# Turning the gated feed-forward rows: VectorE blocks and a DRAM scratch in place of TensorE transposes

## The chip, the core and the metric

One Trainium2 chip, one core. The metric is device time in microseconds (us), the median of the runs of a kernel. The kernel before took 1355.84 us, median of 3 runs (1354.32 to 1356.59).

## The reference, cut to what matters

The model runs two blocks of two layers each on 256 rows of 1024 numbers, all in float32. The change touches the last part of each layer of the second block, the feed-forward:

```python
D_MODEL = 1024; SEQ = 256; DEPTH = 2; D_FF = 2816
def swiglu(h, w_gate, w_up, w_down):
    return (jax.nn.silu(h @ w_gate) * (h @ w_up)) @ w_down
# second block, for l in range(DEPTH), after the mixer has been added to x:
#   x = x + rms_norm_2(swiglu(rms_norm_2(x, ffn_pre[l]), gate[l], up[l], down[l]), ffn_post[l])
```

`silu(h @ w_gate) * (h @ w_up)` is 256 rows by 2816 columns. TensorE sums over the partition axis, so for the product with `w_down` these gated rows have to stand with their 2816 columns on the partitions: they have to be turned.

## The kernel before, in words

**Weights.** TensorE's work is cut into weight units of 4 slices of 128 rows by 512 columns (1 MiB), loaded one after the other by SyncE's queue into a ring of `SLOTS` = 4 places; only the two units of the first group, F0, are staged elsewhere. The load of a unit waits until TensorE has used the unit four places earlier (`w_used`, L590 to L611). ScalarE then rounds a unit in two halves (`round_weights`, L1177), and VectorE subtracts to get the rest of each half (`weight_rests`, L1579). Every product is three matmuls of 512 columns: rounded by rounded, rounded by rest, rest by rounded. One unit is 2 row tiles x 4 slices x 3 = 24 matmuls (L669).

**Feed-forward.** It has 11 groups F0 to F10 (`FF_G` = 11) of two units each: 256 gate columns and 256 up columns, two DMAs of 512 KB to a unit. After group j ScalarE applies silu to the gate half (L1547), VectorE multiplies it with the up half into `sg[:, j % 2]` (L2319), TensorE turns `sg` in four 128x128 transposes into one PSUM bank (step `fh{j}`, L637), ScalarE rounds that bank into `hid_hi[:, j]` (L1538, `turned`) and VectorE writes `hid_rest[:, j]` (`turned_rest`, L1579). The transposes of group j-1 stand between the two units of group j. The groups E0 and E1 (six units each, `w_down`) then multiply `hid_hi` and `hid_rest` by the down weights; unit c of E0 uses what groups 2c and 2c+1 gave.

**Orders.** The order on each engine is written out by hand. In round j ScalarE rounds the weights up to the second unit of group j+1 (`AHEAD` = 2), then does `turned(j-2)`, then silu of group j; VectorE follows with `weight_rests`, `turned_rest(j-2)`, the multiplication. Two pairs of PSUM banks alternate between groups, so group j+2 may start only when group j has been read. SyncE issues the loads in the order of the units, each behind its wait; what stands in its order before a load holds that load back. The first units of F0 and F1 run row tile by row tile, so F0 ends late and F1 5.5 us after it.

Of the kernel before, what the change touches and what calls it, by code (L numbers as in the profile page):

```python
# [7 lines left out]
P = 128  # L8
S = 256
TT = S // P  # L10
D = 1024
KD = D // P
DEPTH = 2
# [7 lines left out]
FF_G = D_FF // 256  # L21
KF = D_FF // P
UNIT_K = 4
SLOTS = 4
# [84 lines left out]
for _n, _name in enumerate(("do_g", "mq_g", "mk_g", "ho_g")):  # L109
# [11 lines left out]
    + ["kT0", "kT1", "mm0", "mm1", "at0", "at1", "mi"] \  # L121
    + [step for n in range(1, len(LEVELS)) for step in [f"Y{n}"] + [f"T{n}"] * (n > 1) + [f"Z{n}"] + BETWEEN.get(n, [])] \
    + ["oT_r0", "oT_r1", "u0", "wT", "st", "vn1", "do0", "do1", "oT_d0", "oT_d1"] \
    + [f"yT{i}" for i in range(4)] + [f"fT{i}" for i in range(4)] + [f"fh{j}" for j in range(FF_G)]
PRE = ["colM", "memT0", "memT1", "memT2", "memT3", "colA", "colB"]
STEPS = PRE + [f"A{l}.{s}" for l in range(DEPTH) for s in ORDER_1] + [f"B{l}.{s}" for l in range(DEPTH) for s in ORDER_2]
STEP_NO = {s: n for n, s in enumerate(STEPS)}
# [57 lines left out]
def parts_until(u):  # L185

    return sum(1 for v, _, _ in PARTS if v <= u)
# [17 lines left out]
def last_unit(group):  # L205
    return max(u for u, (g, _, _) in enumerate(UNITS) if g == GROUP_NO[group])
# [8 lines left out]
def mixer_program(nc, w, out):  # L215
    F = mybir.dt.float32
    FR = mybir.dt.float32r
    ALU = mybir.AluOpType
    ACT = mybir.ActivationFunctionType
    X = mybir.AxisListType.X  # L220
    ctx = ExitStack()
    with ctx:
# [3 lines left out]
        def sem(name):  # L226
            return ctx.enter_context(nc.semaphore(name))
# [39 lines left out]
        def region(at, *shape):  # L267
            n = int(np.prod(shape))
            assert at + n <= ARENA
            v = arena[:, at:at + n]  # L270
            if len(shape) == 1:
                return v
            names = "abcd"[:len(shape)]
            return v.rearrange(f"p ({' '.join(names)}) -> p {' '.join(names)}",
                               **{c: s for c, s in zip(names[:-1], shape[:-1])})
# [36 lines left out]
        R2 = {g: 1024 * n for n, g in enumerate(names_2)}  # L312
# [5 lines left out]
        b_tmp, b_mx, b_pw, b_gf = take(1024), take(1024), take(512), take(1024)  # L318
# [23 lines left out]
        xs2 = region(b_e, TT, D)  # L342
        sq2 = region(b_e, 2048)
        sg = region(b_tmp, 2, 2, S)


        def part(name, at, *shape):
# [20 lines left out]
        hid_hi, hid_rest = part("hid_hi", R2["RV"], FF_G, 2, S), part("hid_rest", R2["RV"] + FF_G * 2 * S, FF_G, 2, S)  # L368
# [40 lines left out]
        pow_asked, pow_given = sem("pow_asked"), sem("pow_given")  # L409
        v_chain, a_chain = sem("v_chain"), sem("a_chain")  # L410
        out_done = sem("out_done")
        w_rounded, w_split = sem("w_rounded"), sem("w_split")
        named = {}
        pow_widths = []

        def sig(name):
            if name not in named:
                named[name] = sem(name)
            return named[name]

        def computed(step):
            return step_done, STEP_NO[step] + 1

        def read_out(step):
            return step_read[STEP_NO[step] % 4], STEP_NO[step] // 4 + 1

        def bank(step, *dims):
            v = mp[:, STEP_NO[step] % 4]
            if len(dims) == 2:
                n = dims[0] * dims[1]  # L430
                return v[:, 0:n].rearrange("p (a b) -> p a b", a=dims[0])
            return v[:, 0:dims[0]] if dims else v
# [10 lines left out]
        def taken(group):  # L443
            return group_read[GROUP_NO[group] % 2], GROUP_NO[group] // 2 + 1
# [99 lines left out]
        def load_signal(u):  # L544
            return staged_loaded[staged_half(u)] if u in STAGED_UNITS else w_loaded[slot_of(u)]

        def load_place(u):
            return ("staged", staged_half(u)) if u in STAGED_UNITS else ("ring", slot_of(u))

        place_total = collections.Counter()  # L550
        unit_value = []
        for u in range(len(UNITS)):
# [4 lines left out]
        def _(sp):  # L557
# [6 lines left out]
            for u in range(1, len(UNITS)):  # L564
# [23 lines left out]
                if u in STAGED_UNITS:  # L588
                    l, g = int(GROUPS[UNITS[u][0]][0][1]), GROUPS[UNITS[u][0]][0][3:]
# [19 lines left out]
                    sp.dma_start(const[:, c0:c1], w["shape_constants"][:, c0:c1]).then_inc(loaded["const2"], 16)  # L609
                for dst, src in unit_loads(u):  # L610
                    sp.dma_start(dst, src).then_inc(load_signal(u), 16)  # L611
            for t in range(TT):
                sp.wait_ge(sig("x_tile"), 2 * (3 * DEPTH) - TT + t + 1)
                sp.dma_start(out[0, t * P:(t + 1) * P, :], x[:, t, :]).then_inc(out_done, 16)
# [4 lines left out]
        def _(pe):  # L619
# [14 lines left out]
            def transposes(step, tiles, *waits):  # L634
                begin(step, *waits)
                for j, tile in enumerate(tiles):
                    last = nc.tensor.transpose(bank(step)[:, P * j:P * j + P], tile, ident)  # L637
                end(last)
# [34 lines left out]
            def split_units(group, count, halfway=None, tile_ready=None):  # L673

                for _ in range(count):
                    u = state["unit"]
                    g, k0, _ = UNITS[u]
                    assert GROUPS[g][0] == group
                    state["unit"] += 1
                    if k0 == k_ends(group)[0] and g >= 2:  # L680
                        pe.wait_ge(group_read[g % 2], g // 2)
                    for n in range(parts_until(u - 1), parts_until(u)):
                        if halfway is not None and n > parts_until(u - 1):
                            halfway()
                        split_part(n, range(TT), tile_ready).then_inc(w_used, 1)
# [240 lines left out]
            for l in range(DEPTH):  # L926
                s = lambda n: f"B{l}.{n}"

                def group_in(g):
                    n = GROUP_NO[s(g)]  # L930
                    return group_read[n % 2], n // 2 + 1
# [169 lines left out]
                                   (1, 1, "halfway"): lambda: tile_transposes(s("fT"), DEPTH + 2 * l + 1, 0)})  # L1101
                rows_first(s("fT"), DEPTH + 2 * l + 1)

                def hid_transposes(j):
                    transposes(s(f"fh{j}"), [sg[:, j % 2, t, P * c:P * c + P] for c in range(2) for t in range(TT)], group_in(f"F{j}"))
                hid_transposes(0)
                split_units(s("F2"), 1)
                hid_transposes(1)
                split_units(s("F2"), 1)
                for j in range(3, FF_G):  # L1110
                    split_units(s(f"F{j}"), 1)
                    hid_transposes(j - 1)
                    split_units(s(f"F{j}"), 1)
                for c in range(-(-KF // UNIT_K)):
                    for j in range(2 * c, min(2 * (c + 1), FF_G)):
                        pe.wait_ge(*read_out(s(f"fh{j}")))
                    split_units(s("E0"), 1)
                    if c == 0:
                        hid_transposes(FF_G - 1)
                split_units(s("E1"), -(-KF // UNIT_K) - SLOTS)  # L1120
                split_tail(SLOTS, {(1, 2, "halfway"): lambda: tile_transposes(f"B{l + 1}.xT", DEPTH + 2 * l + 2, 0)} if l + 1 < DEPTH else {})
            assert state["unit"] == len(UNITS) and state["step"] == len(STEPS)
# [3 lines left out]
        def _(act):  # L1126
# [243 lines left out]
            for l in range(DEPTH):  # L1370
# [163 lines left out]
                result((s("M0"), s("M1")), DEPTH + 2 * l, next_units(s("F0")),  # L1534
                       lambda t: h_round(s("fT"), col("ffn_pre", l), t, hT_hi))
                def turned(j):
                    act.wait_ge(*computed(s(f"fh{j}")))
                    nc.scalar.activation(hid_hi[:, j], bank(s(f"fh{j}"), 2, S), ACT.Copy).then_inc(sig("turned"), 1)  # L1538
                for j in range(FF_G):
                    round_weights(parts_until(last_unit(s(f"F{j}")) + AHEAD))  # L1540
                    if j > 1:
# [5 lines left out]
                        ins = nc.scalar.activation(sg[:, j % 2, t], group_bank(s(f"F{j}"), t)[:, 0:S], ACT.Silu, scale=row_scale[:, t:t + 1])  # L1547
                    ins.then_inc(sig("ff_sig"), 1)
                turned(FF_G - 2)
                turned(FF_G - 1)  # L1550
                round_weights(parts_until(last_unit(s("E1"))))
                if l + 1 < DEPTH:
# [7 lines left out]
        def _(dve):  # L1560
# [7 lines left out]
            def evac(ins, step):  # L1568
                ins.then_inc(step_read[STEP_NO[step] % 4], 1)
                dve.wait_ge(*read_out(step))  # L1570
# [7 lines left out]
            def sub(o, i0, i1):  # L1578
                return nc.vector.tensor_tensor(o, i0, i1, ALU.subtract)  # L1579
# [17 lines left out]
            def weight_rests(count):  # L1597
                while halved[0] < count:
                    u, k, nk = PARTS[halved[0]]
                    dve.wait_ge(w_rounded, halved[0] + 1)  # L1600
                    sub(rest_of(u)[:, k:k + nk, :], raw_of(u)[:, k:k + nk, :], rounded_part(u)[:, k:k + nk, :].bitcast(F))\
                        .then_inc(w_split, 1)
                    halved[0] += 1
# [426 lines left out]
            for l in range(DEPTH):  # L2030
# [275 lines left out]

                def turned_rest(j):
                    dve.wait_ge(sig("turned"), FF_G * l + j + 1)
                    evac(sub(hid_rest[:, j], bank(s(f"fh{j}"), 2, S), hid_hi[:, j].bitcast(F)), s(f"fh{j}"))
                for j in range(FF_G):  # L2310
                    n = s(f"F{j}")
                    weight_rests(parts_until(last_unit(n) + AHEAD))
                    if j > 1:
                        turned_rest(j - 2)
                    dve.wait_ge(sig("ff_sig"), FF_G * l + j + 1)
                    if j == 0:
                        dve.wait_ge(sig("x_normed"), 2 * (DEPTH + 2 * l + 1) + TT)
                    for t in range(TT):
                        ins = nc.vector.scalar_tensor_tensor(sg[:, j % 2, t], group_bank(n, t)[:, S:2 * S], row_scale[:, t:t + 1],  # L2319
                                                             sg[:, j % 2, t], ALU.mult, ALU.mult)  # L2320
                    ins.then_inc(group_read[GROUP_NO[n] % 2], 1)
                    dve.wait_ge(*taken(n))
                turned_rest(FF_G - 2)
                turned_rest(FF_G - 1)
                weight_rests(parts_until(last_unit(s("E1"))))

# [40 lines left out]
```

## Time and profile before

| what | value |
|---|---|
| median of 3 runs | 1355.84 us |
| profiled execution, span from first to last instruction | 1352.6 us |
| TensorE matmul busy | 1340.9 us (99%) |
| VectorE busy | 935.8 us (69%) |
| ScalarE busy | 746.4 us (55%) |
| DMA, mean busy share of 16 engines | 0.51, 167 GB/s |
| TensorE's granted clock | 0.999 of full speed |

The profile page gives for the profiled execution the span and no other time; the median of the runs lies 3.2 us above it. Busy time of matmuls has modelled ends; for the pace of TensorE the starts are what counts. The chain of work that ended last is followed back from the last instruction, and its pieces are given in order of time.

### The profile page before, as it was taken

How to read it: one execution, taken by the hardware profiler on the slowest of the kernel's cores; microseconds unless marked ns; L12 is line 12 of the kernel's file. 1: busy time of each engine (PE TensorE's matmuls, PEld its weight loads, DVE VectorE, ACT ScalarE, POOL GpSimd, SP SyncE). 2: the span in 40 equal slices, each digit the busy share in tenths (PEclk: the TensorE clock that was granted, in tenths of full speed). 3: DMA queues.
4: the chain of work that ended last, by engine and by line, in shares of the span. 5: the costliest groups of instructions: out<-in, count | busy, mean ns of one | idle time of the engine just before them, and what ended most of it. 6: DMA issues, size and time to landing. Idle time of an engine off the chain costs nothing.

```text
span 1352.6 us, 17955 instructions
## 1 busy us (share of the span) xinstructions
PE 1340.9 (99%) x7129; PEld 1146.8 (85%) x7129; DVE 935.8 (69%) x1214; ACT 746.4 (55%) x1067; POOL 58.2 (4%) x44
## 2 busy tenths in 40 slices
PE   9999999999999999999999999999999999999998
PEld 7988888978888998888878888889888887888886
DVE  6789866699867488757885555457695778655544
ACT  6864766675674565544465444456644445544432
POOL 1002000001100001000000000000100000000000
PEclk9999999999999999999999999999999999999999
DMA  8654235554345455434464655644644345466552
GB/s 292 216 168 156 94 125 187 178 165 156 109 148 181 160 198 174 156 118 150 156 218 128 186 186 171 233 156 160 207 156 136 128 157 187 137 206 187 187 176 104
DMA packets 139715, 226.25 MB, mean 167 GB/s; under 512 B 8113, under 2 KB 54897, under 8 KB 139505
## 3 DMA queue, kind: packets, MB, share of 16 engines
q1 hardware_dynamic: 137968, 222.49, 50.1%
q10 hardware_dynamic: 1664, 2.63, 0.5%
q8 instruction: 57, 0.93, 0.3%
q14 instruction: 26, 0.21, 0.1%
HBM read 224.05 MB, written 1.05 MB: 166 GB/s over the span
## 4 chain that ended last, share of the span: by engine, by line
PE 95%; DVE 2%; ACT 1%; issue 1%; DMA 0%; SPq 0%; ACTq 0%; DVEq 0%
PE gp L669 73%; PE gp L657 8%; PE mp L637 5%; PE mp L982 3%; PE mp L798 1%; DVE wt_rest L1579 1%; PE mp L865 1%; PE mp L840 1%; PE mp L975 1%; PE mp L819 1%; PE mp L826 1%; ACT first_hi L1177 1%; DMA wt<-in_w_mem_kv 0%; DVE arena L1573 0%; DVE arena L1576 0%
## 5 line engine op out<-in xcount | busy, mean ns | idle before, releaser
L1579 DVE TENSOR_TENSOR wt_rest<-wt,wt_hi 128x1024 fp32r<-128x1024 f32 x148 | 174.4, 1221 | 83.0 <-ACT wt_hi L1177 81.3
L1177 ACT ACTIVATE wt_hi<-wt 128x1024 fp32r<-128x1024 f32 x148 | 148.1, 1053 | 97.1 <-DMA wt<-in_ffn_down 48.5
L1177 ACT ACTIVATE mix_hi<-wt 128x1024 fp32r<-128x1024 f32 x128 | 132.1, 1060 | 103.7 <-PE gp L669 74.7
L1579 DVE TENSOR_TENSOR wt_rest<-wt,mix_hi 128x1024 fp32r<-128x1024 f32 x128 | 151.1, 1221 | 35.1 <-ACT mix_hi L1177 34.1
L1579 DVE TENSOR_TENSOR wt_rest<-wt,first_hi 128x1024 fp32r<-128x1024 f32 x104 | 124.0, 1221 | 25.8 <-ACT first_hi L1177 24.9
L669 PE MATMUL gp<-mix_hi,mix_hT_hi 128*128 128x512 f32 x352 | 139.9, 397 | 0.0
L669 PE MATMUL gp<-wt_rest,mix_hT_hi 128*128 128x512 f32 x352 | 137.1, 390 | 0.0
L669 PE MATMUL gp<-mix_hi,mix_hT_rest 128*128 128x512 f32 x352 | 133.4, 390 | 0.0
L669 PE MATMUL gp<-wt_hi,hT_hi 128*128 128x512 f32 x320 | 126.7, 396 | 0.0
L1177 ACT ACTIVATE first_hi<-wt 128x1024 fp32r<-128x1024 f32 x104 | 105.8, 1059 | 36.9 <-PE gp L669 26.1
L669 PE MATMUL gp<-wt_hi,hT_rest 128*128 128x512 f32 x320 | 124.9, 390 | 0.0
L669 PE MATMUL gp<-wt_rest,hT_hi 128*128 128x512 f32 x320 | 124.6, 389 | 0.0
L2344 POOL TENSOR_TENSOR rs_out<-rs_in,minus_half 128x1 f32<-128x1 f32 (+3 forms) x35 | 53.8, 1539 | 1289.5 <-DVE rs_in L1584 1289.5
L1137 ACT ACTIVATE arena<-gp 128x1024 f32<-128x1024 f32 x50 | 51.3, 1026 | 95.3 <-PE gp L669 95.3
L669 PE MATMUL gp<-first_hi,first_hT_hi 128*128 128x512 f32 x256 | 103.4, 404 | 0.2 <-DVE wt_rest L1579 0.2
L669 PE MATMUL gp<-first_hi,first_hT_rest 128*128 128x512 f32 x256 | 99.9, 390 | 0.0
L669 PE MATMUL gp<-wt_rest,first_hT_hi 128*128 128x512 f32 x256 | 99.8, 390 | 0.0
L669 PEld LDWEIGHTS gp<-mix_hi,mix_hT_rest 128*128 128x128 f32 x352 | 66.1, 188 | 14.1
L669 PEld LDWEIGHTS gp<-mix_hi,mix_hT_hi 128*128 128x128 f32 x352 | 66.2, 188 | 13.5 <-DVE wt_rest L1579 0.8
L669 PEld LDWEIGHTS gp<-wt_rest,mix_hT_hi 128*128 128x128 f32 x352 | 66.2, 188 | 12.7
L637 PE MATMUL mp<-const,arena 128*128 128x128 f32 x568 | 75.5, 276 | 0.6 <-DVE arena L1576 0.4
L637 PEld LDWEIGHTS mp<-const,arena 128*128 128x128 f32 x568 | 66.4, 142 | 10.6 <-issue 3.0
(347 smaller groups left out, 2933.6 us busy)
## 6 DMA issues: line engine op xcount, KB each, us to landing
wt<-in_w_in SPq DMA_DIRECT2D x96, 1024.0 KB, 5.1
wt<-in_w_out SPq DMA_DIRECT2D x20, 1024.0 KB, 5.1
wt<-in_ffn_gate SPq DMA_DIRECT2D x40, 512.0 KB, 4.0
wt<-in_ffn_up SPq DMA_DIRECT2D x40, 512.0 KB, 5.0
wt<-in_ffn_down SPq DMA_DIRECT2D x20, 1024.0 KB, 5.1
wt<-in_w_mem_kv SPq DMA_DIRECT2D x7, 1024.0 KB, 5.2
arena<-in_w_in SPq DMA_DIRECT2D x4, 1024.0 KB, 8.1
wt<-in_w_branch_pool SPq DMA_DIRECT2D x4, 1024.0 KB, 5.0
```

Source lines behind the costliest of these rows:

```text
L637: last = nc.tensor.transpose(bank(step)[:, P * j:P * j + P], tile, ident)
L657: last = nc.tensor.matmul(o, a[:, k, P * c:P * c + P], b[:, :, k0 + k, :], start=(k0 + k == 0 and c % 2 == 0 and i == 0), stop=(k0 + k == ...
L669: last = nc.tensor.matmul(group_bank(group, t), a, b[:, k, :], start=(kk == k_first and i == 0), stop=(kk == k_last and i == 2))
L798: last = nc.tensor.matmul(bank(step)[:, P * h:P * h + P], keys(h), queries(h), start=True, stop=True)
L819: end(nc.tensor.matmul(b[:, P:3 * P], QT[:, h, P:S], KT[:, h // 2, :], start=True, stop=True))
L826: last = nc.tensor.matmul(bank(s(f"ms{h}"), TT, MEM)[:, t, :].rearrange("p (a b) -> p a b", a=TT), reg("A", "QM")[:, t, P * h:P * h + P], ...
L840: last = nc.tensor.matmul(bank(s(f"om{t}"))[:, P * h:P * h + P], mprT[:, h, 2 * t + st, :], reg("A", "VM")[:, st, P * h:P * h + P], start= ...
L982: last = nc.tensor.matmul(bank(step)[:, P * h:P * h + P], lhs(h), rhs(h), start=True, stop=True)
L1137: nc.scalar.activation(dst, group_banks(name), func).then_inc(group_read[GROUP_NO[name] % 2], 1)
L1177: nc.scalar.activation(rounded_part(u)[:, k:k + nk, :], raw_of(u)[:, k:k + nk, :], ACT.Copy)\
L1579: return nc.vector.tensor_tensor(o, i0, i1, ALU.subtract)
L2344: nc.gpsimd.tensor_tensor(rs_out[:, at:at + width], rs_in[:, at:at + width], minus_half[:, 0:width], ALU.pow)\
```

## The change

The 11 steps `fh{j}` of each layer go, with their four TensorE transposes each. In their place, for each group j of a layer:

- VectorE, after its multiplication, turns `sg[:, j % 2]` (128 by 512) in blocks of 32 by 32 into `turned_h[:, j % 2]` with one instruction.
- SyncE writes `turned_h` (256 KB) to `hid_far` in DRAM in rows of 512 bytes, waits for that, and issues four reads of 64 KB that bring the blocks to their places in `hid_raw[:, j]`, in pieces of 128 bytes. All this stands in SyncE's order right behind the load of the second unit of group j+2.
- ScalarE and VectorE take their rounding and rest from `hid_raw` in SBUF. The rest is written over `hid_raw`.
- E0's unit c waits for VectorE's rests (`hid_split`). For the last group both engines first do the weights of two more units.

```diff
+        turned_h = region(b_mx, 2, 2, TT, P)
+        hid_raw = region(R2["RV"] + FF_G * 2 * S, FF_G, 2, S)
+        hid_far = nc.dram_tensor("hid_far", (DEPTH * FF_G, 2 * TT, P, P), F, kind="Internal").ap()
...
+        hid_after = {last_unit(f"B{l}.F{j}") + SLOTS: FF_G * l + j for l in range(DEPTH) for j in range(FF_G)}
...
                 for dst, src in unit_loads(u):
                     sp.dma_start(dst, src).then_inc(load_signal(u), 16)
+                if u in hid_after:
+                    n = hid_after[u]
+                    l, j = divmod(n, FF_G)
+                    sp.wait_ge(sig("hid_turned"), n + 1)
+                    sp.dma_start(hid_far[n].rearrange("m q c -> q m c"), turned_h[:, j % 2].rearrange("q c t i -> q (c t) i"))\
+                        .then_inc(hid_out, 16)
+                    sp.wait_ge(hid_out, 16 * (n + 1))
+                    far = hid_far[n].rearrange("m (p i) (j r) -> j i (m p) r", p=4, j=4)
+                    near = hid_raw[:, j].rearrange("q c s -> q (c s)").rearrange("q (b r) -> q b r", r=32)
+                    for q in range(4):
+                        sp.dma_start(near[32 * q:32 * q + 32], far[q]).then_inc(hid_back, 16)
...
-                hid_transposes(0)
-                split_units(s("F2"), 1)
-                hid_transposes(1)
-                split_units(s("F2"), 1)
-                for j in range(3, FF_G):
-                    split_units(s(f"F{j}"), 1)
-                    hid_transposes(j - 1)
-                    split_units(s(f"F{j}"), 1)
+                for j in range(2, FF_G):
+                    split_units(s(f"F{j}"), 2)
                 for c in range(-(-KF // UNIT_K)):
-                    for j in range(2 * c, min(2 * (c + 1), FF_G)):
-                        pe.wait_ge(*read_out(s(f"fh{j}")))
+                    pe.wait_ge(sig("hid_split"), FF_G * l + min(2 * (c + 1), FF_G))
                     split_units(s("E0"), 1)
-                    if c == 0:
-                        hid_transposes(FF_G - 1)
...
                 def turned(j):
-                    act.wait_ge(*computed(s(f"fh{j}")))
-                    nc.scalar.activation(hid_hi[:, j], bank(s(f"fh{j}"), 2, S), ACT.Copy).then_inc(sig("turned"), 1)
+                    act.wait_ge(hid_back, 16 * 4 * (FF_G * l + j + 1))
+                    nc.scalar.activation(hid_hi[:, j], hid_raw[:, j], ACT.Copy).then_inc(sig("turned"), 1)
...
                 turned(FF_G - 2)
+                round_weights(parts_until(last_unit(s(f"F{FF_G - 1}")) + SLOTS))
                 turned(FF_G - 1)
...
-                    evac(sub(hid_rest[:, j], bank(s(f"fh{j}"), 2, S), hid_hi[:, j].bitcast(F)), s(f"fh{j}"))
+                    sub(hid_rest[:, j], hid_raw[:, j], hid_hi[:, j].bitcast(F)).then_inc(sig("hid_split"), 1)
...
                     dve.wait_ge(*taken(n))
+                    if FF_G * l + j > 1:
+                        dve.wait_ge(hid_out, 16 * (FF_G * l + j - 1))
+                    nc.vector.transpose(turned_h[:, j % 2].rearrange("q c t i -> q t c i"), sg[:, j % 2].rearrange("q t (c i) -> q t c i", c=2))\
+                        .then_inc(sig("hid_turned"), 1)
                 turned_rest(FF_G - 2)
+                weight_rests(parts_until(last_unit(s(f"F{FF_G - 1}")) + SLOTS))
                 turned_rest(FF_G - 1)
```

## Rows read from the trace of the kernel before

**Rows 1.** The page: busy time by engine, and the chain's shares by engine.
```profile
PE 1340.9 (99%) x7129; PEld 1146.8 (85%) x7129; DVE 935.8 (69%) x1214; ACT 746.4 (55%) x1067; POOL 58.2 (4%) x44
...
PE 95%; DVE 2%; ACT 1%; issue 1%; DMA 0%; SPq 0%; ACTq 0%; DVEq 0%
```

**Rows 2.** The chain in order of time, layer 0's feed-forward: start us, us, what.
```profile
724.70 0.44 PE mp L637 x4
...
742.42 10.94 PE gp L669 x48
753.36 0.44 PE mp L637 x4
...
832.89 0.44 PE mp L637 x4
833.33 46.74 PE gp L669 x206
```

**Rows 3.** Timeline of SyncE's queue, same stretch: start us, us, engine line, DMA.
```profile
722.00 0.37 SPq L611 DMA_DIRECT2D wt<-in_ffn_gate  x1
...
724.73 0.37 SPq L611 DMA_DIRECT2D wt<-in_ffn_gate  x1
...
730.66 0.37 SPq L611 DMA_DIRECT2D wt<-in_ffn_gate  x1
...
736.57 0.37 SPq L611 DMA_DIRECT2D wt<-in_ffn_gate  x1
...
747.94 0.37 SPq L611 DMA_DIRECT2D wt<-in_ffn_gate  x1
748.35 0.51 SPq L611 DMA_DIRECT2D wt<-in_ffn_up  x1
```

**Rows 4.** Timeline of ScalarE, same stretch, with idle time before and its releaser.
```profile
719.29 0.84 ACT L1547 ACTIVATE arena<-gp,small 128x256 f32<-128x256 f32 x2 [5.28 <-PE gp L669]
...
736.58 0.84 ACT L1547 ACTIVATE arena<-gp,small 128x256 f32<-128x256 f32 x2 [3.65 <-PE gp L669]
...
742.01 2.01 ACT L1177 ACTIVATE wt_hi<-wt 128x1024 fp32r<-128x1024 f32 x2 [2.70 <-DMA wt<-in_ffn_up]
```

**Rows 5.** Timeline of VectorE, the multiplication of group 2.
```profile
737.52 0.88 DVE L2319 SCALAR_TENSOR_TENSOR arena<-gp,small,arena 128x256 f32<-128x256 f32 x2 [3.04 <-ACT arena L1547]
```

**Rows 6.** VectorE's groups by form: count | busy us, mean ns of one | idle before.
```profile
L1579 DVE TENSOR_TENSOR wt_rest<-wt,wt_hi 128x1024 fp32r<-128x1024 f32 x148 | 174.4, 1221 | 83.0 <-ACT wt_hi L1177 81.3 <-DVE arena L2319 0.4
...
L2319 DVE SCALAR_TENSOR_TENSOR arena<-gp,small,arena 128x256 f32<-128x256 f32 x44 | 19.3, 479 | 67.1 <-ACT arena L1547 67.1
...
L1579 DVE TENSOR_TENSOR hid_rest<-mp,hid_hi 128x512 fp32r<-128x512 f32 x22 | 15.1, 685 | 8.1 <-ACT hid_hi L1538 8.1
```

**Rows 7.** The DMA view of 748 to 753 us: rate in 40 slices of 0.125 us.
```profile
GB/s 0 0 0 0 0 0 0 25 82 74 8 41 33 16 131 279 369 336 336 385 385 385 385 385 385 377 385 385 385 377 393 393 385 377 352 303 148 58 25 8
```

**Rows 8.** Stretches: us, busy by engine, clock, DMA share, GB/s: queued loads; output store.
```profile
725.00:729.00 4.00, 4.00 (x20) 3.29 (x19) 1.98 (x4) 2.12 (x4) 0.00 (x0) 1.00 1.06 357
...
1341.00:1342.00 1.00, 1.00 (x7) 0.81 (x6) 0.00 (x0) 0.00 (x0) 0.00 (x0) 1.00 1.00 410
```

**Rows 9.** Page, DMA issues: count, KB each, median us from issue to landing.
```profile
wt<-in_ffn_up SPq DMA_DIRECT2D x40, 512.0 KB, 5.0
...
out<-x SPq DMA_DIRECT2D x2, 512.0 KB, 2.6
```

**Rows 10.** The two loads of w_ba: second issue in the queue's timeline, then their landings.
```profile
29.49 0.43 SPq L587 DMA_DIRECT2D w_ba<-in_w_in  x1
...
DMA to landing us min/median/max: 2.8/5.0/7.2
```

**Rows 11.** The DMA view of 26.9 to 27.6 us, then of 30.5 to 32 us.
```profile
DMA packets 955, 0.07 MB, mean 99 GB/s; under 512 B 937, under 2 KB 954, under 8 KB 955
...
q1 hardware_dynamic: 955, 0.07, 92.2%
...
q1 hardware_dynamic: 1245, 0.09, 73.2%
```

More of the change, by code:

```diff
@@ L123 @@
     + ["oT_r0", "oT_r1", "u0", "wT", "st", "vn1", "do0", "do1", "oT_d0", "oT_d1"] \
-    + [f"yT{i}" for i in range(4)] + [f"fT{i}" for i in range(4)] + [f"fh{j}" for j in range(FF_G)]
+    + [f"yT{i}" for i in range(4)] + [f"fT{i}" for i in range(4)]
 PRE = ["colM", "memT0", "memT1", "memT2", "memT3", "colA", "colB"]
@@ L411, in mixer_program @@
         out_done = sem("out_done")
+        hid_out, hid_back = sem("hid_out"), sem("hid_back")
         w_rounded, w_split = sem("w_rounded"), sem("w_split")
@@ L1102, in _ @@
                 rows_first(s("fT"), DEPTH + 2 * l + 1)
-                def hid_transposes(j):
-                    transposes(s(f"fh{j}"), [sg[:, j % 2, t, P * c:P * c + P] for c in range(2) for t in range(TT)], group_in(f"F{j}"))
-                hid_transposes(0)
-                split_units(s("F2"), 1)
-                hid_transposes(1)
-                split_units(s("F2"), 1)
-                for j in range(3, FF_G):
-                    split_units(s(f"F{j}"), 1)
-                    hid_transposes(j - 1)
-                    split_units(s(f"F{j}"), 1)
+                for j in range(2, FF_G):
+                    split_units(s(f"F{j}"), 2)
                 for c in range(-(-KF // UNIT_K)):
-                    for j in range(2 * c, min(2 * (c + 1), FF_G)):
-                        pe.wait_ge(*read_out(s(f"fh{j}")))
+                    pe.wait_ge(sig("hid_split"), FF_G * l + min(2 * (c + 1), FF_G))
                     split_units(s("E0"), 1)
-                    if c == 0:
-                        hid_transposes(FF_G - 1)
                 split_units(s("E1"), -(-KF // UNIT_K) - SLOTS)
```

## The prediction

> **What bounds the kernel now.** I read the page first, then the chain of waits in order of time through one feed-forward, then the timelines of SyncE's queue, ScalarE and VectorE over the same stretch, last the DMA views. The page says that TensorE is the bound: busy 99% of the span, and 95% of the chain that ended last [rows 1]. The chain through the feed-forward shows nothing but matmuls and, once a group, a piece of 0.44 us for four transposes; no wait of TensorE stands in it [rows 2]. So a TensorE instruction removed here is time removed, provided that its weights still come in time. The reader is to see two things: what a block of transposes costs in pace, and how much air SyncE's queue and the DMA engines have, for they take over the work.
>
> **What is removed.** 48 matmuls take 48 x 46.74/206 = 10.89 us where nothing stands between them (the long piece of E0 and E1), and a group with its transposes takes 10.94 + 0.44 = 11.38 us, from 742.42 to the next group's 753.79 [rows 2]. One block so costs 0.44 (its piece) to 0.49 (the difference of the groups); I take 0.47. There are 11 a layer, the first at 724.70 and the last at 832.89 [rows 2], 22 in all: 22 x 0.47 = 10.4 us, all on the path. The waits of E0 for what was turned were not on the chain and get looser or tighter without a cost, as shown below.
>
> **What VectorE gets.** One instruction of 128x512 a group. The trace has no such operation; the nearest rows are the subtraction of 128x512 at 0.685 us and that of 128x1024 at 1.221 [rows 6]. I take 0.7, by the size; 1.2 is the other end. VectorE had over 2 us of idle before its multiplication and more before the weights' rests [rows 5, 6], so 22 x 0.7 = 15 us vanish beside TensorE. What matters is when it ends: silu starts at the group's end, the multiplication ends 1.82 us later (736.58 to 737.52 + 0.88) [rows 4, 5], the turn at +2.6. ScalarE's and VectorE's rounding and rest keep their size; that they read SBUF now is worth nothing I can see, 0 to 0.1 us each, off the path.
>
> **What SyncE's queue gets, and who waits for it.** This is the dear part. For each group: the wait for the turn, a write of 256 KB (512 packets of 512 B, 32 an engine), the wait for its landing, four reads (2048 packets of 128 B, 128 an engine). Queued behind them on SyncE is the load of group j+3's first unit, due at half of group j+1 (before: 722.00, 724.73, 730.66, 736.57 [rows 3]), then its second unit, then the next write. Since write and reads wait for a landing and SyncE does nothing else meanwhile, the feed-forward gets a second pace: the cycle from the landing of one write to that of the next. TensorE needs 10.89 us a group. The terms of the cycle, in one line of DMAs:
>
> - From issue to first data: 0.95 us (issued 747.94, first slice with data the eighth of 748 to 753 [rows 3, 7]).
> - The four reads. The smallest packets in the trace are those of w_ba: rows of 8 numbers, 32 B, 1024 a load. In a full queue 955 packets took 0.922 x 16 x 0.7 = 10.3 us of engine, 10.8 ns each; in the second stretch 0.732 x 16 x 1.5 = 17.6 us for 1245, 14.1 ns [rows 11]. A 1 KB packet in a full queue moves at 357 GB/s, 1024 x 16/357 = 45.9 ns [rows 8]. So a 128 B packet lies between 10.8 and 45.9 ns. I take 15, near the row of small packets, with room for its 96 B more (4 ns at the full rate): 128 x 15 = 1.9 us. Issuing four takes 4 x (0.43 + 0.05) = 1.9 us by w_ba's second issue, which had landed 2.8 us after [rows 10]. Issue and data overlap all but the last: 2.5 us. Ends: 1.9 and 5.9.
> - Two units of weights: 2.1 MB at 357 GB/s [rows 8], 5.9 us. A lone unit is worse (its two DMAs ramp up for 1.9 us [rows 7]), but these stand in a full queue.
> - The write: 512 B packets, between 10.8 and 45.9 ns, so 0.35 to 1.5 us; I take 31 ns, 1.0 us. Landing after its last data: the output's store of 512 KB lands at 2.6 us [rows 9], of which 0.52/0.41 = 1.3 is data [rows 8] and 0.95 start: 0.4.
> - Handing over between waits: 0.1.
>
> Sum: 0.95 + 2.5 + 5.9 + 1.0 + 0.4 + 0.1 = 10.85 us, beside TensorE's 10.89. With both low ends it is 9.6, with both high ends 14.75. So by my values the cycle just keeps up, and the result hangs on a few tenths of a microsecond.
>
> The Trainium skill gives a reason against the 15 ns: DMA: Bandwidth & Descriptors, section Specifications, names 512 B as the smallest transfer for line rate and says that below it the engine reads, modifies and writes. The rows of w_ba show packets of 32 B into SBUF without a price of that kind, so on them the trace does not agree; a 128 B one is in no row. What it would cost is a rival below.
>
> **The margin at the start.** F0's silu starts at 719.29 [rows 4], its turn ends at about 721.9, and SyncE sits in that wait while F1's loads' places come free: group 3's units go out at 726.1 and 727.1 where it was 722.00 and 724.73. The first write has the queue to itself: 0.95 + 1.0 + 0.4, landed at 724.2. The next lands one cycle later, 724.2 + 10.85 = 735.1. From a write's landing to group j+3's first half ready: 0.95 + 2.5 + 2.95 (one unit) + 0.8 (landing after data: 753.35 by issue and 5.0 [rows 3, 9], data until 752.6 [rows 7]) + 1.0 rounding (half of 2.01 [rows 4]) + 1.22 rest [rows 6] + 0.1 = 9.5 us. So group 4 is ready at 744.6. TensorE, without transposes, starts group 2 at 724.7 and group 4 at 746.5: 1.9 us of margin. Group 3: 724.2 + 9.5 = 733.7 against 735.6, the same 1.9. In the E0 stage the same rule holds until its fifth unit, which stands behind the last reads; after it SyncE is free. So for a cycle c the loss of a layer is about 11 x (c - 10.87) - 1.9 us, where positive: nine cycles of drift, the first cycle, and the part of c in the 9.5. It starts at c = 11.04 and eats the 5.2 us gain of a layer at c = 11.5.
>
> **What else is late.** silu of group j stands behind the rounding of group j+1's second unit and behind turned(j-2). The unit lands about 1 us before the write of j-1 does (0.9 us of write data and 0.4 landing less its own 0.8), its rounding, rest, the multiplication and the turn take some 5.7 us, and the next write's turn in the queue comes 9.3 us after the landing: 3 us of air. The reads of j-2 land a cycle earlier: no wait. The last group's come about 10 us after TensorE's F10 ends and are ready at +12; E0 wants them in its sixth unit, at 5 x 5.45 = +27. Nothing is lost there. If they came over 15 us later it would cost their excess.
>
> **The sum.** In the profiled execution's terms 1352.6 - 10.4 = 1342.2 us of span; the runs' median lies 3.2 above the span, so 1345.4. For drift in some groups I add 0.6: **1346 us**. Its own range is 1344.5 (a block at 0.49 and noise) to 1350 (c = 11.25, 2.3 lost a layer).
>
> **Rivals.**
> 1. *SyncE's round trip paces the feed-forward: slower than before.* Place: TensorE waits for the weights' rests at the start of groups 5 to 10 and of E0's units. It decides from c = 11.5. Price at c = 12.2, which is 128 B packets at 22 ns and a write of 1.4 us: 11 x 1.33 - 1.9 = 12.7 a layer, 25.5 - 10.4 = 15 slower: 1371 us. For it: SyncE's waits in series, and w_ba's second load, at 1.4 us for half as many packets. Against: the small packets at 10.8 ns when queued, and that DMA is busy for only about 0.6 of a group now.
> 2. *Nearly as rival 1, but short of it:* c from 11.25 to 11.5, 1350 to 1356 us.
> 3. *Packets of 128 B cost what 1 KB ones do,* 45.9 ns, and the write too: c = 14.75, 11 x 3.88 - 1.9 = 40.8 a layer, 81.6 - 10.4 = 71 slower, 1427 us. Against: 10.8 ns for smaller ones. This is what the rule of the skill's page on transfers below 512 B would come to.
> 4. *The transposes go and the time does not:* matmuls around them get slower by as much, 1356 us. Against: 48 matmuls without a block run at 10.89 in the same trace.
>
> **Chances.** Forecast 0.45, rival 2 0.15, rival 1 0.30, rival 3 0.05, rival 4 0.05. 0.2% is 2.7 us, about what a measurement can tell from no change: faster is below 1353.1 and takes the forecast and two thirds of rival 2, 0.55; the same takes the rest of it, rival 4 and the edge of rival 1 (c up to 11.63), 0.13; slower 0.32. The range, 1344.5 to 1369, leaves out rival 3 and the worse half of rival 1.
>
> **What would show it.** In the chain, pieces of 96 and more matmuls without a break and 10.9 us from one silu to the next: the removal. In SyncE's timeline the distance of two writes to the scratch: 10.9 by the forecast, over 11.5 by rival 1, and then idle time of TensorE put down to VectorE's rests in groups 4 to 10. Landing of the reads: 3 to 4 us from the first one's issue; over 6 speaks for rival 3. VectorE's turn: 0.7 us. The forecast is wrong if the cycle is longer than 11.3 us or the write's landing takes over 2 us beyond its place in the queue.

## The result and the profile after

The changed kernel takes 1361.91 us, median of 4 runs (1357.51 to 1362.32), beside 1355.08 for the kernel before (1353.99 to 1356.59) in the same job: ratio 1.0046, 95% interval 1.0034 to 1.0059. It is slower by 0.5%, where 0.7% faster was forecast. In a second job it took 1358.75 us, median of 6 runs (1358.34 to 1359.23), ratio 1.0032, interval 1.0020 to 1.0045. So its slowdown is 6.8 us in one job and 4.4 in the other.

The page after, to be read beside [rows 1]: span, busy times, and the chain's shares.

```profile
span 1360.4 us, 17863 instructions
...
PE 1336.7 (98%) x7041; PEld 1137.8 (84%) x7041; DVE 949.9 (70%) x1236; ACT 746.8 (55%) x1067; POOL 58.2 (4%) x44
...
PE 79%; DMA 10%; DVE 4%; SPq 3%; ACT 2%; issue 1%; ACTq 0%; DVEq 0%
```

88 matmuls are gone (7129 to 7041), as the change says. But the chain no longer runs through TensorE alone: 10% of it is DMA and 3% SyncE's queue, where both had 0% [rows 1]. The chain in order of time shows where. Two cycles of layer 0 (start us, us, what):

```profile
754.67 6.38 DMA hid_far<-arena
...
761.07 0.33 SPq L627
...
763.56 0.49 SPq L616
...
765.19 7.97 DMA wt<-in_ffn_up
...
773.18 1.07 ACT wt_hi L1182
...
774.27 2.23 DVE wt_rest L1585 x2
...
776.55 0.68 DVE hid_rest L1585
777.23 0.80 DVE arena L2325 x2
778.06 0.72 DVE arena L2331
...
778.80 7.00 DMA hid_far<-arena
```

Before there were 10.94 us of matmuls and 0.44 of transposes in turn [rows 2]. Now the chain of layer 0's feed-forward goes round a ring without TensorE in it, from 719.90 to 832.15 us: landing of a write, four reads (L627), loads of weights (L616), landing, rounding, rest, the multiplication, the turn (L2331), the next write. That is rival 1. VectorE's turn stands in this ring, but it does not set the pace: the write that follows it lands 6.38 and 7.00 us after its issue, where the first one, with nothing queued before it, landed 2.28 us after (722.45 to 724.73), and in e2 below the same turn stands before the same write and TensorE waits for nothing. Two lines from the waits of the whole execution (waiting engine <- releaser: us in total, times, longest us) say what TensorE and SyncE waited for:

```profile
PE gp L685 <- DVE wt_rest L1585: 14.4, 18, 2.3
...
SPq L627 <- DMA hid_far<-arena: 134.3, 22, 7.7
```

SyncE stood 134 us in its 22 waits for a write, with loads behind them. Against e2 below, matmul for matmul, TensorE falls 9.4 us behind in the feed-forward and down groups of layer 0 and 8.2 us in those of layer 1, and 1.3 us in all the rest. SyncE's timeline in layer 0, beside [rows 3]:

```profile
722.45 0.37 SPq L621 DMA_DIRECT2D hid_far<-arena  x1
724.75 1.94 SPq L627 DMA_DIRECT2D arena<-hid_far  x4
726.73 0.49 SPq L616 DMA_DIRECT2D wt<-in_ffn_gate  x1
...
738.14 1.92 SPq L627 DMA_DIRECT2D arena<-hid_far  x4
...
749.79 1.92 SPq L627 DMA_DIRECT2D arena<-hid_far  x4
...
761.07 2.44 SPq L627 DMA_DIRECT2D arena<-hid_far  x4
...
844.27 1.92 SPq L627 DMA_DIRECT2D arena<-hid_far  x4
```

The reads start when a write has landed, so their distance is the cycle: (844.27 - 724.75)/10 = 11.95 us in layer 0, and 11.85 in layer 1 (1187.67 to 1306.12), mean 11.90, against 10.85 forecast and TensorE's 10.89. Single cycles run from 11.0 to 13.7 us.

### The profile page after: what moved, and what is told of

Its sections match the earlier page's. It is cut to its first block, busy times and chain, and to the rows that moved or that the text cites. A ratio compares the mean times of both kernels' runs of the same rounds, so it can differ in the third digit from the quotient of the medians.

```text
span 1360.4 us, 17863 instructions
## 1 busy us (share of the span) xinstructions
PE 1336.7 (98%) x7041; PEld 1137.8 (84%) x7041; DVE 949.9 (70%) x1236; ACT 746.8 (55%) x1067; POOL 58.2 (4%) x44
## 4 chain that ended last, share of the span: by engine, by line
PE 79%; DMA 10%; DVE 4%; SPq 3%; ACT 2%; issue 1%; ACTq 0%; DVEq 0%
PE gp L685 57%; PE gp L673 8%; DMA hid_far<-arena 5%; PE mp L653 4%; DMA wt<-in_ffn_up 4%; PE mp L998 3%; DVE wt_rest L1585 2%; SPq L627 2%; PE mp L814 1%; SPq L616 1%; DMA wt<-in_ffn_down 1%; PE mp L881 1%; ACT wt_hi L1182 1%; PE mp L856 1%; DMA wt<-in_w_mem_kv 1%
## 5 line engine op out<-in xcount | busy, mean ns | idle before, releaser
L685 PE MATMUL gp<-wt_hi,hT_hi 128*128 128x512 f32 x320 | 126.1, 394 | 10.2 <-DVE wt_rest L1585 10.0
L685 PEld LDWEIGHTS gp<-wt_hi,hT_hi 128*128 128x128 f32 x320 | 60.1, 188 | 27.8 <-issue 15.9
L685 PE MATMUL gp<-wt_hi,hid_hi 128*128 128x512 f32 x176 | 69.1, 393 | 2.2 <-DVE wt_rest L1585 2.2
```

What stands on the lines that cost most here:

```text
L685: last = nc.tensor.matmul(group_bank(group, t), a, b[:, k, :], start=(kk == k_first and i == 0), stop=(kk == k_last and i == 2))
```

## The experiments

The kernels ran in three jobs, each with the kernel before beside them; its median was 1354.2 to 1354.4 us in each, so times are compared across them. "Span" is that of the profiled execution. "Cycle" is the mean distance between the first reads after one write and those after the next, over both layers, from the profile, as above. Where it is under TensorE's 10.89 us, TensorE sets the pace and the cycle does not.

| kernel | us | ratio, 95% interval | span, us | cycle, us |
|---|---|---|---|---|
| changed, again (a2) | 1358.75 | 1.0032 (1.0020 to 1.0045) | 1356.9 | 11.73 |
| e1 no DMA path | 1344.11 | 0.9925 (0.9910 to 0.9939) | 1341.6 | none |
| e2 wait and reads later | 1343.57 | 0.9919 (0.9902 to 0.9935) | 1341.5 | 10.45 |
| e3 reads in 512 B | 1352.35 | 0.9985 (0.9975 to 0.9994) | 1349.3 | 11.40 |
| e4 one read | 1343.80 | 0.9919 (0.9905 to 0.9934) | 1341.9 | 10.51 |
| e5 path beside transposes | 1359.10 | 1.0036 (1.0023 to 1.0050) | 1357.1 | 11.75 |
| e6 only reads later | 1351.97 | 0.9983 (0.9974 to 0.9992) | 1350.7 | 11.36 |
| e7 reads in 64 B | 1379.10 | 1.0183 (1.0168 to 1.0198) | 1378.6 | 12.62 |
| e8 blocks on the write | 1348.64 | 0.9960 (0.9947 to 0.9974) | 1346.1 | 11.14 |
| e9 e6, weights first | 1350.73 | 0.9973 (0.9962 to 0.9984) | 1350.4 | 11.34 |
| e2 again (b4), 5 rounds | 1344.05 | 0.9924 (0.9911 to 0.9936) | 1342.2 | 10.45 |

My theory: the load of group j+3 stands on SyncE behind a write's landing and four reads, and this series is the pace. The rival: the DMA engines carry too much in the feed-forward, wherever the wait stands. A second rival: the price of small packets.

**e1, the saving alone.** VectorE turns straight into `hid_raw`; the write, the wait for it and the four reads are left out.

```diff
-                if u in hid_after:
-                    ...                          # the write, the wait and the four reads
-                    act.wait_ge(hid_back, 16 * 4 * (FF_G * l + j + 1))
+                    act.wait_ge(sig("hid_turned"), FF_G * l + j + 1)
-                    nc.vector.transpose(turned_h[:, j % 2]...)
+                    nc.vector.transpose(hid_raw[:, j].rearrange("q c (t i) -> q t c i", t=TT), ...)
```

> VectorE turns straight into hid_raw; the write to DRAM and the four reads are left out, so the blocks are not permuted and the output is not the reference's. This prices the removed transposes alone. Theory (series wait: the load of group j+3 stands on SyncE behind a write's landing and four reads) and its rival (the DMA engines carry too much, wherever the wait stands) both say that TensorE's 22 blocks x 0.47 us are gained in full: 10.4 us under the kernel before, 1344.7 us, 1343.5 to 1346, no wait of TensorE for the rests in the feed-forward. A third theory, that matmuls lose what the transposes gave, says 1355.

Measured 1344.11 us, as expected, 10.2 under the kernel before. The price of 0.47 us a block held, and the 22 turns on VectorE took nothing of it back. Rival 4, that the matmuls lose what the transposes gave, falls.

**e2, the wait behind the next load.** The same traffic in the same groups.

```diff
                     sp.dma_start(hid_far[n]...).then_inc(hid_out, 16)
+                if u - 1 in hid_after:
+                    n = hid_after[u - 1]
+                    j = n % FF_G
                     sp.wait_ge(hid_out, 16 * (n + 1))
                     far = hid_far[n]...
```

> As the changed kernel with all of its traffic; only the wait for the write's landing and the four reads move on SyncE behind the load of group j+3's first unit. Series wait: that load goes out at its old time, the margin no longer shrinks, the full gain returns: 1345 to 1347 us, TensorE waits under 1 us in all in the feed-forward. Rival, load of the DMA engines: the same bytes and packets meet in the same groups, so it stays at 1358 to 1362 us with TensorE waiting some 12 us.

Measured 1343.57 us: as fast as without the path, and 1.4 us under the expectation of 1345 to 1347. The expectation stood on the forecast's full gain of 1345.4 us, which was too high (see "From span to time" below). The chain of e2 is one piece again through layer 0's feed-forward:

```profile
719.88 130.33 PE gp L688 x575
```

The DMA share of a stretch there is higher than in the changed kernel, not lower. The view by stretches (stretch; its length; busy us of PE, PEld, DVE, ACT, POOL; clock; DMA share; GB/s) of e2, then of the changed kernel over one cycle:

```profile
749.00:760.00 11.00, 11.00 (x50) 9.13 (x49) 6.91 (x9) 5.26 (x7) 0.00 (x0) 1.00 0.85 241
```

```profile
749.79:761.07 11.28, 11.04 (x49) 8.87 (x48) 6.82 (x8) 5.24 (x8) 0.00 (x0) 1.00 0.80 232
```

With the DMA engines 85% busy TensorE waits for nothing, with 80% it does. The rival falls: it was the order on SyncE. SyncE's timeline in e2:

```profile
748.50 0.37 SPq L621 DMA_DIRECT2D hid_far<-arena  x1
751.41 0.37 SPq L616 DMA_DIRECT2D wt<-in_ffn_gate  x1
751.82 0.51 SPq L616 DMA_DIRECT2D wt<-in_ffn_up  x1
752.38 3.09 SPq L630 DMA_DIRECT2D arena<-hid_far  x4
```

The load goes out when TensorE frees its place (751.41), between the write and the wait.

**e3 and e4, shorter behind the landing.** e3 keeps four reads, in pieces of 512 B; e4 makes one read of all 128 partitions.

```diff
-                    far = hid_far[n].rearrange("m (p i) (j r) -> j i (m p) r", p=4, j=4)
-                    near = hid_raw[:, j].rearrange("q c s -> q (c s)").rearrange("q (b r) -> q b r", r=32)
+                    far = hid_far[n].rearrange("m (j i) c -> j i m c", j=4)                                  # e3
+                    near = hid_raw[:, j].rearrange("q c s -> q (c s)").rearrange("q (m c) -> q m c", c=P)      # e3 and e4
-                    for q in range(4): ...                                                                   # e4
+                    sp.dma_start(near, hid_far[n].rearrange("m q c -> q m c")).then_inc(hid_back, 16)        # e4
```

> The four reads stay four DMAs of 64 KB, but in pieces of 512 bytes instead of 128, so 512 packets a group instead of 2048; the blocks are not permuted and the output is not the reference's. Series wait: issuing four takes 1.9 us still, so the reads end only about 0.5 us earlier and the cycle goes from 11.8 to 11.3: 2 layers x 11 x 0.5 = 11 us less, but not below the full gain, so 1350 to 1354 us. Rival, the small packets are the cost: 1345 to 1347 us, as e4.

> One read of 256 KB over 128 partitions in pieces of 512 bytes in place of the four; the blocks are not permuted and the output is not the reference's. Series wait: the load behind it goes out 1.45 us earlier and the read's data ends 1.6 us earlier, cycle 10.2, shorter than TensorE's 10.89: full gain, 1345 to 1347 us. Small packets as the cost: the same as e3. Load of the DMA engines: as e3 too, since the packets are the same.

Measured 1352.35 us, inside the expectation, and 1343.80 us, 1.2 under it like e2: the full gain. The changed kernel (1358.75) is 15.2 us slower than e2. A quarter of the packets in four DMAs gives back 6.4 of these; the same packets in one DMA give back 15.0. So four DMAs of 32 partitions in place of one of 128 cost at least 8.5 us, more than the packets; at least, because TensorE sets the pace in e4. The rival of small packets alone, 1345 to 1347 us for e3, falls.

**e5, the path beside the transposes.** The kernel before with the new path added; the diff is that of the change without its lines on TensorE, and `turned` waits for both:

```diff
                     act.wait_ge(*computed(s(f"fh{j}")))
+                    act.wait_ge(hid_back, 16 * 4 * (FF_G * l + j + 1))
```

> The kernel before with all its transposes on TensorE, and beside them the whole new path (VectorE's turn, the write, the wait, the four reads), whose data is thrown away: hid_hi and hid_rest come from PSUM as before, but wait for the reads too. Series wait: SyncE's cycle of 11.9 us paces the feed-forward whatever TensorE does in it; against TensorE's 11.36 a group the drift is 9 x 0.54 + 2 x 1.05 = 7.0, less a margin of 3.3, 3.7 us a layer: 1360 to 1364 us, like the changed kernel. Rival, the path costs TensorE a fixed 18 us (what it cost the changed kernel) by load and contention: 1372 us.

> The changed kernel again on this chip, for comparison with the three beside it: 1357 to 1362 us by every theory.

Measured 1359.10 and 1358.75 us, the latter the changed kernel in the same job. 22 blocks of transposes more on TensorE, worth 10.2 us by e1, and the time is the same: what sets the pace is SyncE's cycle (11.75 and 11.73), and TensorE fills its own waits. The rival of a fixed 18 us, 1372, falls. The expectation of 1360 to 1364 was missed by 0.9 us; it had taken a cycle of 11.9. TensorE's waits for the rests are 10.5 us in the changed kernel's second profile, and in e5:

```profile
PE gp L685 <- DVE wt_rest L1597: 2.8, 6, 0.7
```

**e6, only the reads behind the load.** The wait for the landing stays in front of it.

```diff
                     sp.wait_ge(hid_out, 16 * (n + 1))
+                if u - 1 in hid_after:
+                    n = hid_after[u - 1]
+                    j = n % FF_G
                     far = hid_far[n]...
```

> The wait for the write's landing stays in front of the load of group j+3's first unit; only the four reads move behind that load. Tells which half of what stood before the load costs. Series wait: the cycle is still about 11.2 us, but the unit is ready 2 us earlier after the landing, so the margin lasts through the 11 groups: 1344 to 1347 us. If the wait for the landing is the dear half, the reads' place changes little: 1352 to 1358.

Measured 1351.97 us: a miss, I had taken the wait alone for harmless. Of the 15.2 us between the changed kernel and e2, moving the reads gives back 6.8, and moving the wait as well the other 8.4. The cycle was 11.36, not 11.2; and ScalarE now waits for the second unit, which comes behind the reads (ScalarE's timeline of e6, idle before in brackets):

```profile
755.39 2.01 ACT L1185 ACTIVATE wt_hi<-wt 128x1024 fp32r<-128x1024 f32 x2 [3.42 <-DMA wt<-in_ffn_up]
760.09 2.01 ACT L1185 ACTIVATE wt_hi<-wt 128x1024 fp32r<-128x1024 f32 x2 [2.69 <-DMA wt<-in_ffn_up]
```

The two are 4.7 us apart, against 2.9 in the changed kernel (757.48 and 760.36).

**e7, twice the packets.** The reads in pieces of 64 B; the data lands in other places.

```diff
+                    far = hid_far[n].rearrange("m q c -> (m q c)").rearrange("(b q i r) -> q i b r", q=4, i=32, r=16)
+                    near = hid_raw[:, j].rearrange("q c s -> q (c s)").rearrange("q (b r) -> q b r", r=16)
```

> The reads bring the same bytes in pieces of 64 bytes, 4096 packets a group instead of 2048; the data lands in other places and the output is not the reference's. A packet's price is fixed by the packet (12.5 ns of an engine in the changed kernel), so the reads take 1.6 us longer less what hides behind issue, cycle 11.9 to 12.9 or 13.3: by 22 us for each microsecond of cycle, 1380 to 1392 us. Rival, price by bytes: no change, 1358 to 1363.

Measured 1379.10 us, 0.9 under the expectation: the cycle grew by 0.89 us (11.73 to 12.62) where I had said 1.0 to 1.4. 20.3 us of time for 0.89 of cycle is 23 us for each microsecond, as the prediction's formula has it (22). The price by bytes, 1358 to 1363 us, falls.

**e8, the blocks on the write.** Four writes in pieces of 128 B, one wait, one read.

```diff
+                    far = hid_far[n].rearrange("m (b i) (p r) -> p i (m b) r", b=4, p=4)
+                    near = turned_h[:, j % 2].rearrange("q c t i -> q (c t i)").rearrange("q (b r) -> q b r", r=32)
+                    for q in range(4):
+                        sp.dma_start(far[q], near[32 * q:32 * q + 32]).then_inc(hid_out, 16)
+                    sp.wait_ge(hid_out, 16 * 4 * (n + 1))
+                    sp.dma_start(hid_raw[:, j]..., hid_far[n].rearrange("m q c -> q m c")).then_inc(hid_back, 16)
...
```

> The blocks are permuted by the write instead of the read: four writes of 64 KB in pieces of 128 bytes (2048 packets), one wait, then one read of 256 KB in pieces of 512 bytes. Bytes, packets, the wait and its place are those of the changed kernel; what stands behind the landing is one short read, and the 128-byte packets go into a queue that the weights keep full, where 780 pass in 0.5 us, not 490. Series wait: cycle 0.95 + 0.9 + 6.4 + 1.5 + 0.7 = 10.4 us, under TensorE's 10.89, so the full gain: 1343 to 1346 us. Rival, load of the engines or a price for writing under 512 bytes: 1352 us and more, the write landing over 3 us behind the second unit.

Measured 1348.64 us, cycle 11.14: the right way and 10.1 us under the changed kernel, yet 2.6 above the expectation of 1343 to 1346. In the cycle from 748.29 us ScalarE starts on the first unit at 754.55 and on the second at 757.47, and the write lands at 758.92. So the writes were as quick as thought: they land 1.45 us behind the second unit's, where my terms gave 1.4 and the rival over 3. The first unit came 6.3 us after the read's issue, where they gave 5.9 (see the ramp below). Some cycles are longer for no reason that I found, such as 11.82 us from 780.45 and 12.81 from 814.06; the cycle from 748.29 took 10.63.

**e9, e6 with E0's third unit rounded first.**

```diff
+                round_weights(parts_until(last_unit(s(f"F{FF_G - 1}")) + 3))
                 turned(FF_G - 2)
```

and the same for VectorE's rests.

> e6 (wait before the load, reads behind it) with one more edit: ScalarE and VectorE round E0's third unit before they turn to group 9's rows. In e6 the last wait of layer 1 is TensorE's 1.65 us at 1294.9 us for that unit's rests, held by the reads of group 9 at ScalarE. If e6 stayed above my expectation by that head-of-line wait, this gives 2 to 4 us back: 1348 to 1350 us. If it is the cycle of 11.3 to 11.4 us itself, nothing: 1351 to 1353.

Measured 1350.73 us, between the two expectations and 1.2 below e6, with intervals that overlap (0.9962 to 0.9984, 0.9974 to 0.9992). Inconclusive: what stood first in ScalarE's order is a small part of e6's 8.4 us or none. Where the rest comes from, no run shows.

**e2 again, five rounds.**

> The version with the wait and the reads behind the next load again, in five rounds, as the candidate that beats both kernels: 1343 to 1345 us, ratio to the kernel before 0.992.

Measured 1344.05 us, ratio 0.9924, as expected: 10.2 us faster than the kernel before and 14.7 than the changed one, with the traffic of the changed kernel.

## Why the prediction was wrong

**What held.** The price of the transposes: 10.4 us forecast, 10.2 measured (e1). VectorE's turn: 0.7 us forecast, 0.711 measured, and in the cycle from 749.79 us it ended 4.9 us after the landing (754.65), early enough for its write. In the trace after, by form:

```profile
L2331 DVE STREAM_TRANSPOSE arena<-arena 128x512 f32<-128x512 f32 x22 | 15.7, 711 | 0.8
```

The mechanism that decides held too, a cycle of SyncE beside TensorE's 10.89 us, and its price. For the mean cycle c the formula gives a span of 1342.2 + 22 x (c - 11.04). With the measured cycles it says 1361.1 for the changed kernel (measured 1360.4), 1357.4 for its second profile (1356.9), 1350.1 for e3 (1349.3), 1344.4 for e8 (1346.1) and 1377.0 for e7 (1378.6). It does not hold for e5, where TensorE's pace is another, nor for e6 and e9, where the load stands in front of the reads. It leaves out one small thing: in the second profile TensorE's granted clock is 0.50 (its lower level, 1.2 GHz) from 795.0 to 798.4 us, behind 2.4 us without a new matmul, which costs about 1.7 us. The first profile has no such stretch in the feed-forwards.

**What failed: the cycle's sum, 10.85 us, against 11.90.** I had set it just below the point at which it costs, 11.04, and it was too small. Some 0.4 us of the missing 1.05 is one term, the ramp of the loads; the other 0.6 is cycles longer than the rest, for which the sum had no term. ScalarE's rounding waits for the landing of each unit, so its starts and those of the reads give the parts of seven cycles of layer 0 (738.14 to 820.65). One of them stands here (ScalarE's timeline after):

```profile
757.48 2.01 ACT L1182 ACTIVATE wt_hi<-wt 128x1024 fp32r<-128x1024 f32 x2 [5.17 <-DMA wt<-in_ffn_up]
760.36 2.01 ACT L1182 ACTIVATE wt_hi<-wt 128x1024 fp32r<-128x1024 f32 x2 [0.87 <-DMA wt<-in_ffn_up]
```

With the landings of the writes at 749.79 and 761.07: 7.69 to the first unit, 2.88 more to the second, 0.71 to the write, a short cycle of 11.28. The means of the seven are 7.88, 3.20 and 0.70; my terms gave 7.2 (0.95 + 2.5 + 2.95 + 0.8), 2.95 and 0.6. The step that failed in every cycle is the term of two units of weights at 357 GB/s, 5.9 us, with its reason "but these stand in a full queue". They do not. Three half microseconds of that cycle, from the DMA views of 751.5 to 752, 753 to 753.5 and 755 to 755.5 us:

```profile
DMA packets 500, 0.06 MB, mean 124 GB/s; under 512 B 500, under 2 KB 500, under 8 KB 500
...
q1 hardware_dynamic: 500, 0.06, 78.2%
...
DMA packets 112, 0.07 MB, mean 139 GB/s; under 512 B 50, under 2 KB 112, under 8 KB 112
...
DMA packets 196, 0.19 MB, mean 387 GB/s; under 512 B 7, under 2 KB 196, under 8 KB 196
```

First the reads, then the loads at a third of their rate, and only then a full queue. The reads start in an empty queue at SyncE's issuing pace, 512 packets per 0.53 us. Their last packets pass before 753.5, so their term of 0.95 + 2.5 us held. The loads behind them start slowly (139 GB/s here, 193 in the next half microsecond), as a lone unit does in [rows 7]. This was among my rows, and I set it aside.

The ramp alone would not have made the kernel slower. Nine of the twenty cycles took 11.0 to 11.4 us, mean 11.26. With that cycle the formula gives a span of 1347.0 us (an estimate), and the time is 1.9 above the span: 1349 us, faster than before. What makes it slower is the other eleven, and above all the six of 12.2 to 13.7 us, the first one of layer 0 among them. Where I looked (the cycles from 724.75, 761.07, 785.81 and 820.65) a few packets trail for about 1 us before the landing; the line is that of 772.5 to 773 us:

```profile
DMA packets 18, 0.01 MB, mean 24 GB/s; under 512 B 1, under 2 KB 18, under 8 KB 18
```

In each of the six, issuing one DMA, or one group of four reads, took SyncE 0.5 to 1.2 us longer than the same did elsewhere (the four reads at 820.65 took 3.10 us, those at 749.79 took 1.92), and in none of the nine. But in the second profile two long cycles (12.80 us from 782.87, 12.23 from 795.67) have no such issue. Why the packets trail, and whether the long issues are cause or effect, stays open. So does why the runs of the first job range over 4.8 us and those of the second over 0.9.

**The first cycle.** Forecast to end at 735.1, it ended at 738.14, so the margin of 1.9 us before group 4 was gone at once: TensorE waits 1.3 us there, from 747.0 on. With the mean cycle of each layer, 11.95 and 11.845 us, the formula gives losses of 10.0 and 8.8 us, where TensorE fell 9.4 and 8.2 behind e2. Another 1.3 us were lost elsewhere and bring the sum nearer than its parts are. That is luck.

**From span to time.** The forecast added 3.2 us to the span, the distance between one execution's span and the median of others. Run by run the time lies 1.8 to 1.9 us above the span (1362.32 and 1360.4 for the changed kernel, 1343.31 and 1341.5 for e2; only in e1 it is 2.3). So the full gain is near 1344 us and not 1345.4.

**The 128-byte packets.** Assumed 15 ns of an engine, by [rows 11]; measured 12.5 in the half microsecond from 751.5 (0.782 x 16 x 500 ns / 500 packets), with the engines idle a fifth of the time. In a full queue they pass faster, at 10.5 ns of each engine (16 x 500 ns / 764) and less. The DMA views of 756 to 756.5 us of e2 (reads) and of 757 to 757.5 us of e8 (writes):

```profile
DMA packets 764, 0.13 MB, mean 250 GB/s; under 512 B 747, under 2 KB 763, under 8 KB 763
```

```profile
DMA packets 860, 0.11 MB, mean 214 GB/s; under 512 B 860, under 2 KB 860, under 8 KB 860
```

So rival 3 had no ground: the trace does not agree with the Trainium skill's read-modify-write below 512 B (DMA: Bandwidth & Descriptors, Specifications) as a price in time, neither for reads into SBUF nor, in e8, for writes to DRAM. The same page of the Trainium skill (DMA: Bandwidth & Descriptors, Issuing engines are not separate DMA queues) calls the sequencer's time to start a DMA "usually small relative to the DMA itself". Here it was not: SyncE takes 0.53 us to issue 512 packets, and a full queue moves as many in 0.34 us (512/764 x 0.5).

**The chances.** Rival 1 had 0.30, with 1371 us at c = 12.2; by the same formula c = 11.8 gives 1362, near what was measured. The sum of six terms was 1.05 us off, and 0.65 was enough to eat the whole gain, since 22 us go with each microsecond of it. Slower deserved the larger share.

## What to carry to other kernels

In SyncE's order a wait for one transfer delays all that stands behind it. Before you take such a wait into a queue of loads, put it behind the next load that is due; here that is the whole difference between 0.3 to 0.5% slower and 0.8% faster, with the same bytes. Count a series of DMAs through an emptied queue at the ramp's rate and the issuer's pace, not at the full queue's. Use the mean of such a cycle and not its shortest case (here 11.90 and 11.26 us), and where two paces come out equal, forecast the slower side. Removing work from an engine that another ring paces gives nothing (e5 against the changed kernel): look for the second pace first.

## What the runs showed of the hardware

Packets of 128 bytes are not dear in a full queue: about 0.6 ns each over the 16 engines together (764 read in 0.5 us in e2, 860 written in e8). But into an empty queue, four DMAs of 64 KB bring their 2048 packets no faster than SyncE issues them, in about 2.1 us. A load behind them ran at 139 and 193 GB/s in its first two half microseconds and at 387 in a full queue. A VectorE turn of 128x512 float32 in 32x32 blocks takes 0.711 us, 0.026 more than a subtraction of that size [rows 6].
